# A transformer and mixture-of-experts chain on one core: first loads over two queues, the first projection tile by tile, rotation angles on GpSimd

## What is computed

```python
def rope_tables(positions, dtype):
    inv_freq = ROPE_THETA ** (-jnp.arange(0, DIFF_HEAD_DIM, 2, dtype=jnp.float32) / DIFF_HEAD_DIM)
    ang = positions.astype(jnp.float32)[..., None] * inv_freq
    return (jnp.cos(ang)[:, :, None, None, :].astype(dtype),
            jnp.sin(ang)[:, :, None, None, :].astype(dtype))

def apply_rope(t, cos, sin):
    t1, t2 = jnp.split(t, 2, axis=-1)
    return jnp.concatenate([t1 * cos - t2 * sin, t1 * sin + t2 * cos], axis=-1)
...
        h = rmsnorm(x, norm_mix_g[l])
        proj = h @ w_in[l]
        p, q, k, v = jnp.split(
            proj, [POOL_WIDTH, POOL_WIDTH + ATTN_WIDTH, POOL_WIDTH + 2 * ATTN_WIDTH], axis=-1)
        pool_out = multiscale_pool(p, pool_w[l], pool_scale[l])
        q = apply_rope(q.reshape(b, s, N_DIFF_HEADS, 2, DIFF_HEAD_DIM), cos, sin)
        k = apply_rope(k.reshape(b, s, N_DIFF_HEADS, 2, DIFF_HEAD_DIM), cos, sin)
...
        lam = (jnp.exp(jnp.sum(lambda_q1[l].astype(jnp.float32) * lambda_k1[l].astype(jnp.float32)))
               - jnp.exp(jnp.sum(lambda_q2[l].astype(jnp.float32) * lambda_k2[l].astype(jnp.float32)))
               + lam_init)
        attn_out = diff_attention(q, k, v, lam, lam_init, attn_norm_g[l])
        mix = jnp.concatenate([pool_out, attn_out], axis=-1) @ w_o[l]
```

## Time and profile before

| | us |
|---|---|
| runs | 1043.42, 1044.59, 1044.85 |
| median | 1044.59 |
| the profiled execution | 1044.39 |
| its span, first to last instruction | 1042.6 |
| TensorE busy | 1014.8 |
| VectorE busy | 842.5 |
| ScalarE busy | 665.3 |
| GpSimd busy | 35.3 |

### The profile page before, as it was taken

How to read it: one execution, slowest core, us unless ns; L and a number is a source line. 1 busy time by engine, 2 the same in 40 slices (tenths; PEclk the granted TensorE clock), 3 DMA queues, 4 the chain that set the end, 5 groups by cost and what they waited for, 6 DMA issues and landing times. The chain is left out here.

```text
span 1042.6 us, 14963 instructions
## 1 busy us (share of the span) xinstructions
PE 1014.8 (97%) x5574; PEld 864.6 (83%) x5574; DVE 842.5 (81%) x1091; ACT 665.3 (64%) x836; POOL 35.3 (3%) x43
## 2 busy tenths in 40 slices
PE   7999999999999999989999999999999999999997
PEld 6787999999999788989878778787878787877774
DVE  5855777676677777887869799999999999999977
ACT  5664655555555755566454677777777777777764
POOL 2000000000000100100120000000000000000000
PEclk9999999999999999999999999999999999999999
DMA  9734546465525454342205989898989898999871
GB/s 343 271 121 141 181 166 219 159 205 177 188 86 162 162 177 152 122 151 93 81 33 202 335 318 388 348 382 345 391 345 387 347 386 345 374 362 384 348 308 44
DMA packets 82711, 253.62 MB, mean 243 GB/s; under 512 B 4160, under 2 KB 42176, under 8 KB 62656
## 3 DMA queue, kind: packets, MB, share of 16 engines
q1 hardware_dynamic: 82624, 252.50, 65.0%
HBM read 251.44 MB, written 1.05 MB: 242 GB/s over the span
## 5 line engine op out<-in xcount | busy, mean ns | idle before, releaser
L1072 DVE TENSOR_TENSOR WL<-raw,WH 128x2048 fp32r<-128x2048 f32 x230 | 493.8, 2178 | 91.6 <-ACT WH L547 91.5
L547 ACT ACTIVATE WH<-raw 128x2048 fp32r<-128x2048 f32 x231 | 419.5, 1822 | 126.1 <-PE bank L2014 83.9
L2012 PE MATMUL bank<-WH,MXH 128*128 128x512 f32 x552 | 226.4, 410 | 0.2 <-DVE WL L1072 0.2
L2014 PE MATMUL bank<-WH,MXL 128*128 128x512 f32 x552 | 215.3, 390 | 0.0
L2013 PE MATMUL bank<-WL,MXH 128*128 128x512 f32 x552 | 215.2, 390 | 0.0
L2012 PE MATMUL bank<-HTH,WH 128*128 128x256 f32 x576 | 165.4, 287 | 2.3 <-DVE HTL L1095 1.2
L2013 PE MATMUL bank<-HTL,WH 128*128 128x256 f32 x576 | 163.1, 283 | 0.0
L2014 PE MATMUL bank<-HTH,WL 128*128 128x256 f32 x576 | 163.1, 283 | 0.0
L2012 PE MATMUL bank<-WH,HTH 128*128 128x512 f32 x348 | 139.4, 400 | 4.1 <-DVE WL L1119 2.3
L2013 PE MATMUL bank<-WL,HTH 128*128 128x512 f32 x348 | 135.7, 390 | 0.0
L2012 PEld LDWEIGHTS bank<-WH,MXH 128*128 128x128 f32 x552 | 103.8, 188 | 27.0 <-issue 6.8
(11 more groups left out here) (405 smaller groups left out, 1103.9 us busy)
## 6 DMA issues: line engine op xcount, KB each, us to landing
raw<-in_exp_w_up SPq DMA_DIRECT2D x52, 1024.0 KB, 8.0
raw<-in_exp_w_gate SPq DMA_DIRECT2D x52, 1024.0 KB, 8.2
raw<-in_exp_w_down SPq DMA_DIRECT2D x52, 1024.0 KB, 6.8
raw<-in_w_in SPq DMA_DIRECT2D x34, 1024.0 KB, 5.3
raw<-in_w_up SPq DMA_DIRECT2D x22, 1024.0 KB, 5.4
raw<-in_w_down SPq DMA_DIRECT2D x11, 1024.0 KB, 5.1
raw<-in_w_out SPq DMA_DIRECT2D x8, 1024.0 KB, 5.0
raw<-in_w_o SPq DMA_DIRECT2D x4, 1024.0 KB, 5.7
```

Source lines behind the costliest of these rows:

```text
L547: e.activation(WH[i % HL][:, 0:n], raw[i % RAW][:, 0:n], ACT.Copy).then_inc(a_wh, 1)
L1072: e.tensor_tensor(l, r, h.bitcast(F32), ALU.subtract).then_inc(v_wl, 1)
L2012: e.matmul(out_, ah, bh, start=start, stop=False)
L2014: return e.matmul(out_, al, bh, start=False, stop=stop)
```

## The change

The first transfers. ScalarE issues piece 0 itself, as two halves, at the start of its list; SyncE issues constants, x's first half, `pt`, the positions, piece 1 as two halves, x's second half, and then as before. Each half has a semaphore of its own (`d_first`, `d_raw`).

The columns of x are made per token half. Eight transposes of half 0 go to banks 0 to 3, then eight warming products; the second eight transposes stand inside the query projection. ScalarE's and VectorE's column instructions are 128 columns wide, sixteen of each instead of eight of 256.

Fourteen instructions stand ahead of the first power, where there were none. The core of the diff:

```diff
+        def load_halves(e, i):
+            src = piece_src(a, PIECES[i])
+            dst = raw[i][:, :].rearrange("p (k n) -> p k n", k=4)
+            e.dma_start(dst[:, 0:2, :], src[:, 0:2, :]).then_inc(d_first[i], 16)
+            e.dma_start(dst[:, 2:4, :], src[:, 2:4, :]).then_inc(d_raw[i], 16)
...
-            for t in range(T):
-                e.dma_start(X[:, t, :], a["x"][t * P:(t + 1) * P, :]).then_inc(d_x[t], 16)
+            e.dma_start(X[:, 0, :], a["x"][0:P, :]).then_inc(d_x[0], 16)
             e.dma_start(pt[:, :], a["pt"]).then_inc(d_pt, 16)
-            load_pieces(0, 2)
             e.dma_start(sm[:, 0:2].bitcast(I32), a["positions"]).then_inc(d_pos, 16)
+            load_halves(e, 1)
+            e.dma_start(X[:, 1, :], a["x"][P:2 * P, :]).then_inc(d_x[1], 16)
...
+            load_halves(e, 0)
+            e.wait_ge(d_pt, 16)
...
+            mix_columns(0, 0, 4)
+            first_half(0)
+            mix_columns(0, 4, 6)
+            second_half(0)
+            mix_columns(0, 6, 8)
+            first_half(1)
+            second_half(1)
             e.wait_ge(d_x[0], 16)
             squares("mix", 0, X[:, 0, :], ss[:, 0:1])
...
+            mix_columns(1, 0, 8)
             e.wait_ge(d_x[1], 16)
             squares("mix", 1, X[:, 1, :], ss[:, 1:2])
             split(2)
-            for i, dst in enumerate((sin, cos)):
-                e.wait_ge(v_ang, i + 1)
-                e.activation(dst, dst, ACT.Sin).then_inc(a_rot, 1)
+            e.wait_ge(own_g, G_OWN["angles"])
+            e.activation(sincos, sincos, ACT.Sin).then_inc(a_rot, 1)
             split(3)
...
+            mix_columns(0, 0, 4)
+            first_half(0)
+            mix_columns(0, 4, 6)
+            second_half(0)
+            mix_columns(0, 6, 8)
+            e.wait_ge(d_pos, 16)
+            e.tensor_copy(posf, sm[:, 0:2].bitcast(I32)).then_inc(v_pos, 1)
+            first_half(1)
+            second_half(1)
+            mix_columns(1, 0, 8)
             means("mix")
             split(2)
...
+            split(3)
...
+            turn_mix(0)
+            warm(8, 7)
+            first_q(0, 0)
+            first_q(0, 1)
+            first_q(1, 0)
+            turn_mix(1)
+            first_q(1, 1).then_inc(p_tok0, 1)
+            second_q(0)
+            second_q(1)
```

More of the change, by code:

```diff
@@ L124 @@
 HROW = numbered(["ffn", "n1"])
+G_OWN = numbered(["q0", "q1", "rows", "ang0", "ang1", "turn0", "turn1", "up", "down"]
+                 + [(c, n) for c in range(3) for n in ("part", "rest")] + ["quarter", "angles"])
 TOK0 = numbered(["q", "k", "v", "p", "wo0", "wo1", "fin0", "fin1", "z0", "z1", "v0", "v1", "o0", "o1", "wm0", "wm1", "we0", "we1"])
@@ L1124, in vector, with mix_columns @@
-            columns("mix", "norm_mix_g", 0, (4, 5, 6, 7), HTH, HTL, (2, 3))
-            split(1)
+            def mix_columns(t, k0, k1):
+                for k in range(k0, k1):
+                    ts = slice(t * 128, (t + 1) * 128)
+                    if k % 2 == 0:
+                        e.wait_ge(a_colh, 2 * COL["mix", 4 * t + k // 2])
+                    m = e.scalar_tensor_tensor(out=HTL[:, k, ts], in0=mix_at(t, k), scalar=ptcol("norm_mix_g", k),
+                                               in1=HTH[:, k, ts].bitcast(F32), op0=ALU.mult, op1=ALU.subtract)
+                    if k % 2:
+                        m.then_inc(v_coll, 1)
@@ new lines, in gpsimd @@
+            e.memset(QN[1][0:64, :, :], 0.0).then_inc(own_g, 1)
+            e.wait_ge(own_g, G_OWN["q1"])
+            e.memset(rowsT.bitcast(F32), 0.0).then_inc(own_g, 1)
+            e.wait_ge(own_g, G_OWN["rows"])
+            e.wait_ge(d_cn, 16)
+            e.wait_ge(v_pos, 1)
+            for t in range(T):
+                e.tensor_scalar(ang[:, t, :], const("invf", 32), posf[:, t:t + 1], None, ALU.mult).then_inc(own_g, 1)
+            MAGIC = 12582912.0
+            C1, C2 = 6.28125, 0.0019350051879882812
@@ L2103, in tensor, with turn_mix, first_q, second_q @@
             e.wait_ge(d_cn, 16)
-            columns(X, (4, 5, 6, 7), ((d_x[0], 16), (d_x[1], 16)))
-            warm(9, 0)
+            def turn_mix(t):
+                e.wait_ge(d_x[t], 16)
+                for k in range(8):
+                    m = e.transpose(mix_at(t, k), X[:, t, k * 128:(k + 1) * 128], ident)
+                    if k % 2:
+                        m.then_inc(p_cols, 1)
+            def first_q(kh, c):
+                wh, wl = (v[kh][:, :].rearrange("p (k n) -> p k n", k=4) for v in (WH, WL))
+                ks = (2 * c, 2 * c + 1)
+                e.wait_ge(v_coll, COL["mix", 2 * kh + c])
+                e.wait_ge(a_wh if c else a_w0, kh + 1)
+                for part in (HTH, HTL):
+                    for k in ks:
+                        e.matmul(bank[4][:, :], part[:, 4 * kh + k, 0:128], wh[:, k, :],
+                                 start=(part is HTH and kh == 0 and k == 0), stop=False)
+                e.wait_ge(v_wl if c else v_w0, kh + 1)
+                for k in ks:
+                    m = e.matmul(bank[4][:, :], HTH[:, 4 * kh + k, 0:128], wl[:, k, :], start=False,
+                                 stop=(kh == 1 and k == 3))
+                return m
+            def second_q(kh):
+                wh, wl = piece(kh, 4)
+                for k in range(4):
+                    if k % 2 == 0:
+                        e.wait_ge(v_coll, COL["mix", 4 + 2 * kh + k // 2])
+                    m = three(bank[5][:, :], HTH[:, 4 * kh + k, 128:256], HTL[:, 4 * kh + k, 128:256], wh[:, k, :],
+                              wl[:, k, :], kh == 0 and k == 0, kh == 1 and k == 3)
+                m.then_inc(p_used, 1)
+            turn_mix(0)
[7 more added lines that the diff above has]
+            second_q(1)
             def turn_qk(c):
@@ L2182, in tensor @@
             e.wait_ge(a_pcp, 2)
[L2183 removed]
+            e.wait_ge(d_pool, 32)
             pool_mean(0)
```

145 lines of the change are left out of this document (68 added, 77 removed).

## The result

| | median us | range, runs |
|---|---|---|
| kernel before, beside it | 1044.13 | 1042.95 to 1045.27, 11 |
| changed kernel | 1046.36 | 1045.86 to 1047.25, 11 |

The ratio is 1.0022, with a 95% interval of 1.0014 to 1.003: 2.2 us slower. The prediction was 1045.0, slower by 0.6. The time lies in its range (1042.3 to 1047.2), and just inside the forecast's own span (1044.4 to 1046.4), by 0.04; the angles, at 25.91, lie past that span's condition (23.5 to 25.5). By the bound of 0.2% this is the case "slower", to which it gave 0.13. The profiled execution of the changed kernel took 1046.49, with a span of 1044.3, against 1044.39 and 1042.6.

A forecast was written before the change was run, and what follows sets the result against it. TensorE, busy 97%, bounds the kernel; in the first 45 us the angles, split 3 and rotations come last. Rotations 0.6 us late outweigh TensorE's own 0.6 gain: 1044.39 + 0.6 = 1045.0 us, range 1042.3 to 1047.2.

The forecast's parts named there:

- The path and the yardstick: First 45 us: angles, split 3, rotations set the start of the last key turning, forecast at 43.5 against 42.88.
- angles + 5.45: VectorE's rotations start 5.45 us after the angles, through sine, both splits 3 and lambda sums: 29.55 against 28.97.
- Break-even: Angles ready on GpSimd at 23.5 would leave the yardstick neither earlier nor later.
- The angles at 24.1: GpSimd: 4.5 us of angle work done before low split 2, remaining 1.6 after its end at 22.5.
- x at 6.2: First transfers: sharing the DMA engines row for row with piece 0 lands x at 6.2 instead of 4.8.
- Copies from 7.8: ScalarE's column copies 0 to 3 start at 7.8, when the gains table pt lands.
- Warming 16 passes at 0.12: TensorE: after 8 transposes from 6.2, 16 warming passes at 0.12 us end at 9.8; first useful matmul at 9.9.
- The block of GpSimd: GpSimd stands still while VectorE subtracts two SBUF tensors; without it angles at 19.5. Thin evidence for one-input operations.
- The sum of 6.1 us: GpSimd's 14 angle operations, 5.2 us, plus ten waits at 0.09; cheap end 4.3, dear end 9.2.
- Hidden angles: Rival: GpSimd done before low split 2 at 20.3, both late TensorE gaps (0.99) vanish, 1042.8; chance 0.31.
- GpSimd the bound: Rival: GpSimd's angle work at its dear end, 9.2 us, angles at 27.2, slower at 1048.1; chance 0.13.
- Transfers apart: Rival: second queue doesn't delay x and pt, head up to 2 us earlier, 1040.8 with hidden angles; chance 0.06.

The follow-up runs named there:

- table_early: Changed kernel plus a one-column copy on ScalarE that draws its first table load ahead of the wait for pt: 1046.01 us, ratio 1.0022.
- pos_behind: Changed kernel with the positions' transfer issued by ScalarE behind the two halves of piece 0, no longer by SyncE: 1046.68 us, ratio 1.0024.
- one_queue: Changed kernel with both halves of piece 0 issued by SyncE behind the positions, none by ScalarE: 1045.2 us, ratio 1.0016.
- lambda_first: Changed kernel with the four small lambda sums back ahead of low split 3 on VectorE: 1045.88 us, ratio 1.0022.
- pos_moved: Changed kernel with the positions' transfer issued by ScalarE ahead of the two halves of piece 0, no longer by SyncE: 1045.29 us, ratio 1.0012.
- angles_early: Kernel before with the angles on GpSimd, positions issued by ScalarE at its start and cast as VectorE's first instruction: 1042.19 us, ratio 0.9983.
- cast_first: Changed kernel with the position cast as VectorE's first instruction: 1043.83 us, ratio 1.0004.
- all_four: Changed kernel with piece 0 on SyncE's queue, positions on ScalarE's queue and cast first, lambda sums early, early one-column table-load copy: 1042.23 us, ratio 0.9983.
- three_2q: all_four without its first edit, so piece 0 stays on ScalarE's queue and both queues are in use: 1042.21 us, ratio 0.9985.
- less_warm: three_2q with half the warming products, 8 passes instead of 16: 1042.6 us, ratio 0.999.
- pool_more: Changed kernel plus an unneeded 2048-column memset on GpSimd (1.82 us) in the middle of the angle computation: 1048.91 us, ratio 1.0051.

## Why the prediction was right, and where it was off

**The path and the yardstick: right.** Angles, sine, split 3, low split 3, lambda sums, rotations set the end. The step "angles + 5.45" put the rotations at 31.36 for the measured 25.91; VectorE began them at 31.21. Break-even was put at angles of 23.5; the rule above gives a sine at 42.88 - 19.16 = 23.72. TensorE waited 1.25 for the low split of piece 4 until 38.36 (1.4 near 36 was forecast). Had the angles been put at 25.91, the prediction's own sum would have been 1044.39 + 2.4 = 1046.8.

**The angles at 24.1: off by 1.8, which is more than the whole miss of 1.4.** The prediction made them low split 2's end plus what is then left: the split's start was put at 20.3 and was 22.48, the rest at 1.6 and was 1.2.

Counted from GpSimd's start, the account is simpler. From there to the angles it forecast 13.4 to 24.1, 10.7 us; measured are 15.21 to 25.91, also 10.7. Inside these 10.7 two errors cancel, and that is luck: 6.9 us of work for 6.1, and 3.8 of standing still for 4.6. So the 1.8 is all in the start: the cast at 14.84 for 13.4, and 0.37 from the cast to the first operation, for which the sum had nothing. Other runs with the same GpSimd list bear it out: from GpSimd's first operation to the angles are 10.5 to 10.7 us (14.50 to 25.01 in table_early, 15.16 to 25.65 in pos_behind, 14.02 to 24.52 in one_queue, 15.17 to 25.72 in lambda_first, 13.74 to 24.40 in pos_moved). Low split 2 shifts this only within one operation's length: it began 7.0 us behind GpSimd's start where the chain took 10.5, and 7.3 in the changed kernel. By an estimate from the rows above, a split at 20.3 would have given angles at the same time, near 26, with 3.4 us of work left behind it.

Two terms made the cast late, and a third made TensorE late:
- *x at 6.2* (it came at 7.36). The row-for-row sharing would fit when both transfers are issued together: 5.75 to 6.15 there. The prediction named that ScalarE issues "at once" but gave the 0.44 us of head start no price; pos_behind against pos_moved puts 1.5 us on it, with the rival named there. Here even the bound "byte for byte", 6.6, was too early. The Trainium skill (DMA: Bandwidth & Descriptors, Issuing engines are not separate DMA queues) says that engines' transfers interleave and only the issue time is saved; the traces agree: on one queue x came at 5.12, on two never before 5.75.
- *Copies from 7.8* (9.40). Of the 1.6 us, about 0.9 is pt, which was there at 8.69 in table_early, and 0.7 is the table load, which ran from 8.11 to 9.39. "Table loads on ScalarE lie in its waiting time" was wrong for the first. Before the change the squares of x came first on ScalarE and the load ran at 0.74, free of any wait. Now the first activation is the copy, and the load stands behind that copy's wait for TensorE. The Trainium skill (ScalarE: Activation LUTs, What ACT_TABLE_LOAD costs) gives about 1283 ns for it and about 1380 ns for a drain beside it. The trace agrees with the first (1.28) and shows no drain: the copy began at 9.40, when the load begun at 8.11 was over, and in angles_early the load at 18.16 began when a split ended (16.21 and 1.93) and the sine followed it at 19.45.
- *Warming 16 passes at 0.12* (3.62 in all, 0.23 each). So the first useful matmul began at 12.37, not at 9.9, the three short waits that were forecast never appeared, and TensorE's own stream was 1.4 us late instead of 0.6 early. It delayed the second tile's transposes (17.01 instead of 15.1); ScalarE waited 1.03 us for them, and low split 2 came later by up to that. What the slow passes were worth shows in pos_behind, where x and the cast stand within 0.06 of the changed kernel and the passes took 2.52: low split 2 began 0.32 earlier, the sine came 0.26 earlier. So the slow passes cost this kernel some 0.2 to 0.3; in cast_first they took a part of the gain. In pos_behind the three short waits are there, too: steps of 0.63, 0.61 and 0.69 ahead of the matmuls on a low half (12.75, 14.40, 16.12), where the others are 0.46 to 0.47, so 0.15 to 0.23 each for the 0.3 to 0.5 forecast.

**The cast's place.** The half splits stand right behind it and move with it, so they meet GpSimd's first operation wherever the cast is in time. The one operation that was to "slip in ahead of 1b" did not: the first one stood from 15.21 to 17.49, until both half splits were over (16.04 and 1.21, so 17.25).

**The block of GpSimd: right, and now shown.** The doubt was whether one-input operations are blocked too. They are: 2282 ns against 358 for the same line. The Trainium skill (SBUF — State Buffer, Who interferes with whom) has the rule, and the trace agrees for both kinds of operation. **The sum of 6.1 us** was 6.9 (3.43 to 10.33 unblocked): 128-wide operations with one input take 0.53 to 0.54 and not 0.40 (the last clamp 0.29), two-input ones 0.46.

**The rivals.** "Hidden angles" (1042.8) is what cast_first made: the gaps go but for 0.34, yet without a gain (1043.83), since the late x and the slow warming passes had taken TensorE's share. "GpSimd the bound" has the right sign and the wrong cause: not 9.2 us of work, but 6.9, and a chain of forecast length that began 1.8 late. "Transfers apart" did not happen.

What the change could have been: the angles on GpSimd with the positions fetched at once (angles_early, 1042.19 against 1043.79) beat both kernels; the two queues and the finer first projection add nothing to it that these runs can tell (all_four 1042.23, three_2q 1042.21, less_warm 1042.6).

## What to carry to other kernels

Work that is moved to an idle engine is free only if its input comes early enough and no other engine blocks it meanwhile, as VectorE's splits block GpSimd here: ask first where the value that releases it is made, and put that tiny instruction ahead of everything. A transfer on a second queue delays one that runs beside it (x at 5.75 or later with it, at 5.20 or earlier without), and most where it was issued first: issue it after the one that is needed first. And look at what an engine's first instruction will be after an edit, since a table load goes with it.

## What the runs showed of the hardware

- GpSimd's one-input operations wait out VectorE's subtraction of two SBUF tensors as two-input ones do (358 against 2282 ns at 32 columns), and nothing gets in between splits that follow each other (one operation from 15.21 to 17.49, over splits at 14.90 and 16.04). Where VectorE's `HTL` products stand between two splits, one operation gets done per split (cast_first: 11.59 and 1.52, 13.19 and 1.57, each over one split).
- With 1 MB in two halves on ScalarE's queue issued at 0.74 and 1.24, the 0.5 MB of x issued at 1.18 on the other were used at 7.31; with the halves at 1.18 and 1.67, behind the positions, at 5.80.
- TensorE's first passes differ from kernel to kernel with the same list. The 16 warming passes took 3.62 us in the changed kernel and in pos_moved, but 2.52 and 2.60 in pos_behind and table_early, which began them at 9.04 and 9.22, about as late as the changed kernel (9.10); pool_more, which changes nothing on TensorE, took 2.98. The eight transposes at the start took 1.94, the eight of the second tile at 17.01 took 1.03. The clock column reads 1.00 in all these stretches, the upper level, 2.4 GHz, so by these rows the granted clock doesn't tell the slow passes from the fast ones. What does stays open.
